# Delta rule: level products as pairs of 64x64 quarters of TensorE's array, on packed tiles

## The reference

```
m = where(strict, einsum('bhncd,bhnsd->bhncs', k_beta, k) * decay, 0.0)
t_inv = triangular_solve(eye + m, eye, lower=True, unit_diagonal=True)
u = t_inv @ v_beta
w = t_inv @ (k_beta * exp(g)[..., None])
```

## Time and profile before

| | |
|---|---|
| median of 3 runs | 1583.88 us (1583.28 to 1585.54) |
| profiled execution, own time | 1580.38 us |
| its span, first to last instruction | 1577.5 us |
| TensorE busy, share of the span | 97% |
| VectorE, ScalarE, GpSimd busy | 38%, 38%, 36% |
| granted TensorE clock, mean | 0.997 |

### The profile page before, as it was taken

The page is one execution under the profiler, slowest core; times in us unless marked ns, Lnnn a source line. Parts: engine busy times, 40 slices in busy tenths (PEclk is TensorE's granted clock), DMA queues, the critical chain, the costliest instruction groups (busy, mean ns, idle before and its releaser), DMA issues.

```text
span 1577.5 us, 21190 instructions
## 1 busy us (share of the span) xinstructions
PE 1534.2 (97%) x7900; PEld 1267.5 (80%) x7900; DVE 595.1 (38%) x996; ACT 603.7 (38%) x998; POOL 560.0 (36%) x270
## 2 busy tenths in 40 slices
PE   6889999999999999999999999999999999999998
PEld 6868888888887778888888887777688888888887
DVE  3355556565565422221022224566432222012210
ACT  5643444334442533322232234576433332223221
POOL 4522321323212244434533444221234444444442
PEclk9999999999999999999999999999999999999999
DMA  7411111111110133233323233111123332433322
GB/s 250 125 64 54 41 30 51 54 41 44 38 34 11 50 94 113 88 98 92 117 81 106 82 85 124 48 41 33 36 78 107 109 94 76 124 94 94 90 84 80
DMA packets 39218, 124.41 MB, mean 79 GB/s; under 512 B 4192, under 2 KB 5472, under 8 KB 39136
## 3 DMA queue, kind: packets, MB, share of 16 engines
q1 hardware_dynamic: 38976, 123.01, 25.5%
q10 hardware_dynamic: 160, 0.26, 0.1%
HBM read 120.89 MB, written 2.10 MB: 78 GB/s over the span
## 4 chain that ended last, share of the span: by engine, by line
PE 93%; DVE 3%; ACT 3%; issue 1%; DMA 0%; POOL 0%; SPq 0%; DVEq 0%; ACTq 0%
PE bank L564 72%; PE bank L730 3%; PE bank L717 3%; PE bank L728 2%; ACT ws L1091 2%; PE bank L1025 1%; DVE act_lo L1536 1%; PE bank L892 1%; PE bank L851 1%; DVE ws L1539 1%; PE bank L576 1%; PE bank L1049 1%; PE bank L738 1%; PE bank L881 1%; PE bank L764 1%
## 5 line engine op out<-in xcount | busy, mean ns | idle before, releaser
L511 POOL TENSOR_TENSOR w_lo<-w_raw,w_hi 128x1024 fp32r<-128x1024 f32 (+1 forms) x250 | 539.9, 2175 | 835.3 <-ACT w_hi L1091 835.1
L564 PE MATMUL bank<-act_hi,w_hi 128*128 128x512 f32 (+1 forms) x1776 | 708.3, 399 | 6.7 <-DVE act_lo L1536 2.7
L564 PE MATMUL bank<-act_hi,w_lo 128*128 128x512 f32 (+1 forms) x1776 | 680.1, 383 | 0.0
L564 PE MATMUL bank<-act_lo,w_hi 128*128 128x512 f32 (+1 forms) x1776 | 679.5, 383 | 0.0
L564 PEld LDWEIGHTS bank<-act_hi,w_hi 128*128 128x128 f32 x1776 | 335.4, 189 | 74.7 <-issue 13.5
L564 PEld LDWEIGHTS bank<-act_hi,w_lo 128*128 128x128 f32 x1776 | 334.7, 188 | 65.8
L564 PEld LDWEIGHTS bank<-act_lo,w_hi 128*128 128x128 f32 x1776 | 335.5, 189 | 62.2 <-issue 5.6
L1091 ACT ACTIVATE w_hi<-w_raw 128x1024 fp32r<-128x1024 f32 (+1 forms) x250 | 230.5, 953 | 88.8 <-PE bank L564 86.6
L1530 DVE TENSOR_TENSOR ws<-bank,ws 128x512 f32<-128x512 f32 x110 | 75.9, 690 | 336.2 <-PE bank L564 326.2
L1091 ACT ACTIVATE ws<-ws 128x512 f32<-128x512 f32 (+2 forms) x135 | 87.1, 647 | 154.6 <-DVE ws L1530 107.4
L1798 DVE TENSOR_TENSOR xT<-xT,bank 128x512 f32<-128x512 f32 (+1 forms) x48 | 33.0, 687 | 257.0 <-PE bank L564 257.0
(11 more groups left out here) (150 smaller groups left out, 1218.7 us busy)
## 6 DMA issues: line engine op xcount, KB each, us to landing
w_raw<-w_stream SPq DMA_DIRECT2D x154, 512.0 KB, 3.6
w_raw<-w_out SPq DMA_DIRECT2D x32, 384.0 KB, 3.1
w_raw<-w_down SPq DMA_DIRECT2D x32, 384.0 KB, 3.1
w_raw<-w_down SPq DMA_DIRECT2D x32, 320.0 KB, 3.2
ws<-x_in SPq DMA_DIRECT2D x1, 2048.0 KB, 8.8
ws<-mem_in SPq DMA_DIRECT2D x2, 512.0 KB, 4.7
out<-ws SPq DMA_DIRECT2D x1, 1024.0 KB, 4.2
sq_c<-squares_in SPq DMA_DIRECT2D x1, 768.0 KB, 7.1
```

The lines of the kernel that those rows point to most:

```text
L511: nc.gpsimd.tensor_tensor(w_lo[:, s, 0:width * P], w_raw[:, s, 0:width * P], w_hi[:, s, 0:width * P].bitcast(F32), ALU.subtract).then_inc( ...
L564: mm = nc.tensor.matmul(acc, wt[:, c % RING, wsl], at[:, act0(k0 + k), off:off + n], start=(start and k == 0 and m == 0), stop=(stop and k ...
```

## The change

The lower and upper 64 rows of a tile meet only in the last level. So in levels 1 to 5 M, T and Z of a tile consist of two diagonal blocks of 64x64, and the off-diagonal ones are zero. Now each block is a product of its own, on the quarter of the array that its rows and output rows give: 64 rows, 64 columns of weights and 64 streamed columns. The blocks are kept packed: the row `TT` holds in its first 256 columns the four turned copies, 64 columns each, with the upper block on partitions 0 to 63 and the lower one on 64 to 127, and in its second 256 columns Z in the same form. `PM` is packed likewise. The masks become 64 wide (`small`). The joined Z is written out into `ZZ` in level 5, by row halves. The last level computes only the off-diagonal block of Z, on the quarters off the diagonal (P: rows 0 to 63 to outputs 64 to 127; Z: rows 64 to 127 to outputs 0 to 63). The turned copy comes from products with the identity on quarters instead of transposes. ZZ is cleared once at the start, beside KBG.

In the diff "..." stands for lines that don't change.

```diff
@@ -86,8 +86,10 @@
-(IDENT, ONES, ONES64, TRIU, NEG_LOWER, LEVEL0) = range(6)
-N_SQ = 6 + LEVELS - 1
+HB = P // 2
+(IDENT, ONES, ONES64, TRIU, NEG_LOWER, SMALL) = range(6)
+SMALL_IDENT, SMALL_LEVEL0 = 0, 1
+N_SQ = SMALL + (1 + LEVELS) // 2
@@ -98,10 +100,10 @@
     out[:, NEG_LOWER] = np.where(r <= c, 0.0, -1e30)
-    out[:, LEVEL0] = (c == r + 1) & (r % 2 == 0)
-    for k in range(1, LEVELS):
-        b = 2 ** k
-        out[:, LEVEL0 + k] = (r // b % 2 == 1) & (c // b == r // b - 1)
+    r, c = r % HB, np.arange(HB)[None, :]
+    small = [r == c, (c == r + 1) & (r % 2 == 0)]
+    small += [(r // 2 ** k % 2 == 1) & (c // 2 ** k == r // 2 ** k - 1) for k in range(1, LEVELS - 1)]
+    out[:, SMALL:].reshape(P, -1)[:, 0:HB * len(small)] = np.concatenate(small, axis=1)
     return out
@@ -337,6 +339,24 @@
+        def small(i, tiles):
+            at = SMALL * P + HB * i
+            flat = sq_c[:].rearrange("p a c -> p (a c)")[:, at:at + HB]
+            return flat.unsqueeze(1).to_broadcast([P, tiles, HB])
+        def half_rows(q):
+            return slice(HB * q, HB * (q + 1))
+        def diag(i, t, r, c):
+            return ws[half_rows(r), i, P * t + HB * c:P * t + HB * (c + 1)]
+        def packed(i, t, r, second=0):
+            at = SEQ // 2 * second + HB * t
+            return ws[half_rows(r), i, at:at + HB]
         def over_tiles(i):
@@ -414,6 +434,16 @@
             return act_hi[P // 2 * half:P // 2 * (half + 1), 18, :]
+        PER_HEAD = 2 * (LEVELS - 3) + 3 * 2 + 2
+        def tz_count(k, g, first_only=False):
+            if k < LEVELS - 2:
+                return 2 * (k - 1) + g + 1
+            if k == LEVELS - 2:
+                return 2 * (LEVELS - 3) + 3 * g + (1 if first_only else 3)
+            return 2 * (LEVELS - 3) + 6 + g + 1
@@ -700,7 +730,11 @@
                 pe.wait_ge(S.dm_pre, h + 1)
-                transposes4(D[2], ZZ).then_inc(S.t_tr, 1)
+                for t in range(NT):
+                    for r in range(2):
+                        mm = nc.tensor.matmul(bank[half_rows(r), D[2], HB * t:HB * (t + 1)], packed(TT, t, r, 1),
+                                              sq_c[half_rows(r), IDENT, HB * r:HB * (r + 1)], start=True, stop=True)
+                mm.then_inc(S.t_tr, 1)
                 pe.wait_ge(S.qn_done, h + 1)
@@ -708,14 +742,20 @@
                     n = 12 * h + 2 * (k - 1)
+                    last = k == LEVELS - 1
                     for g in range(2):
...
                         else:
-                            pe.wait_ge(S.tz_done, n + g - 1)
+                            pe.wait_ge(S.tz_done, PER_HEAD * h + tz_count(k - 1, g, last))
                         for i, t in enumerate(half_tiles(g)):
-                            mm = nc.tensor.matmul(bank[:, D[3 - g], i * P:(i + 1) * P], tt(MM, t), tt(TT, t),
-                                                  start=True, stop=True)
+                            if last:
+                                mm = nc.tensor.matmul(bank[half_rows(1), D[3 - g], HB * i:HB * (i + 1)],
+                                                      diag(MM, t, 0, 1), packed(TT, t, 0), start=True, stop=True)
+                                continue
+                            for r in range(2):
+                                mm = nc.tensor.matmul(bank[half_rows(r), D[3 - g], HB * i:HB * (i + 1)],
+                                                      diag(MM, t, r, r), packed(TT, t, r), start=True, stop=True)
                         mm.then_inc(S.p_mm, 1)
@@ -723,16 +763,24 @@
                             pe.wait_ge(S.kdec_done, h + 1)
+                        if last:
+                            pe.wait_ge(S.tz_done, PER_HEAD * h + tz_count(k - 1, g))
                         for i, t in enumerate(half_tiles(g)):
-                            if k < LEVELS - 1:
-                                nc.tensor.matmul(bank[:, D[4 + g], i * P:(i + 1) * P], tt(ZZ, t), tt(PM, t),
-                                                 start=True, stop=True)
-                            mm = nc.tensor.matmul(bank[:, D[4 + g], (2 + i) * P:(3 + i) * P], tt(PM, t), tt(ZZ, t),
-                                                  start=True, stop=True)
+                            z_at = slice(P + HB * i, P + HB * (i + 1))
+                            if last:
+                                mm = nc.tensor.matmul(bank[half_rows(0), D[4 + g], z_at], packed(PM, t, 1),
+                                                      diag(ZZ, t, 1, 1), start=True, stop=True)
+                                continue
+                            for r in range(2):
+                                nc.tensor.matmul(bank[half_rows(r), D[4 + g], HB * i:HB * (i + 1)],
+                                                 packed(TT, t, r, 1), packed(PM, t, r), start=True, stop=True)
+                            for r in range(2):
+                                mm = nc.tensor.matmul(bank[half_rows(r), D[4 + g], z_at], packed(PM, t, r),
+                                                      packed(TT, t, r, 1), start=True, stop=True)
                         mm.then_inc(S.tz_mm, 1)
...
-                pe.wait_ge(S.tz_done, 12 * h + 12)
+                pe.wait_ge(S.tz_done, PER_HEAD * (h + 1))
                 pe.wait_ge(S.kbg_done, h + 1)
@@ -786,7 +834,7 @@
-            pe.wait_ge(S.rw_cols, 5)
+            pe.wait_ge(S.rw_cols, 6)
             pe.wait_ge(S.ba_copied, 1)
@@ -1254,11 +1302,11 @@
                 a(psum(D[0]), w(E0), ACT.Exp, scale=-0.5, bias=col("ln_q")).then_inc(S.rr_done, 1)
-                act.wait_ge(S.z_pre, h + 1)
+                act.wait_ge(S.z_pre, 2 * h + 2)
                 a(w(MM), psum(D[1]), ACT.Copy).then_inc(S.t_done, 1)
...
                 act.wait_ge(S.t_tr, h + 1)
-                a(w(TT), psum(D[2]), ACT.Copy).then_inc(S.t_done, 1)
+                a(w(TT)[:, 0:SEQ // 2], psum(D[2], SEQ // 2), ACT.Copy).then_inc(S.t_done, 1)
                 if due(h):
@@ -1627,7 +1675,8 @@
             V.memset(w(KBG), 0.0).then_inc(S.rw_cols, 1)
-            dve.wait_ge(S.rw_cols, 1)
+            V.memset(w(ZZ), 0.0).then_inc(S.rw_cols, 1)
+            dve.wait_ge(S.rw_cols, 2)
             dve.wait_ge(S.ba_g, 1)
@@ -1667,9 +1716,15 @@
                 dve.wait_ge(S.mt_done, h + 1)
-                mul(psum4(D[3]), psum4(D[1]), over_tiles(LEVEL0)).then_inc(S.z_pre, 1)
-                dve.wait_ge(S.z_pre, h + 1)
-                sub(w4(ZZ), over_tiles(IDENT), psum4(D[3])).then_inc(S.z_done, 1)
+                pair_c = "p (t c) -> p t c"
+                for r in range(2):
+                    own = half_rows(r)
+                    mul(bank[own, D[3], 0:SEQ // 2].rearrange(pair_c, t=NT),
+                        bank[own, D[1], :].rearrange(pair_c, t=NT)[:, :, HB * r:HB * (r + 1)],
+                        small(SMALL_LEVEL0, NT)[own]).then_inc(S.z_pre, 1)
+                dve.wait_ge(S.z_pre, 2 * h + 2)
+                sub(w(TT)[:, SEQ // 2:].rearrange(pair_c, t=NT), small(SMALL_IDENT, NT),
+                    psum(D[3], SEQ // 2).rearrange(pair_c, t=NT)).then_inc(S.z_done, 1)
                 dve.wait_ge(S.rr_done, 2 * h + 2)
@@ -1680,19 +1735,30 @@
                         dve.wait_ge(S.p_mm, n + g + 1)
-                        own = slice(SEQ // 2 * g, SEQ // 2 * (g + 1))
-                        mul(w(PM)[:, own].rearrange("p (t c) -> p t c", c=P),
-                            bank[:, D[3 - g], 0:SEQ // 2].rearrange("p (t c) -> p t c", c=P),
-                            sq_c[:, LEVEL0 + k:LEVEL0 + k + 1, :].to_broadcast([P, NT // 2, P])).then_inc(S.p_done, 1)
+                        own = slice(P * g, P * (g + 1))
+                        if k < LEVELS - 1:
+                            mul(w(PM)[:, own].rearrange(pair_c, c=HB), psum(D[3 - g], P).rearrange(pair_c, c=HB),
+                                small(SMALL_LEVEL0 + k, NT // 2)).then_inc(S.p_done, 1)
+                        else:
+                            cp(ws[HB:, PM, own], bank[HB:, D[3 - g], 0:P]).then_inc(S.p_done, 1)
                     for g in range(2):
                         dve.wait_ge(S.tz_mm, n + g + 1)
-                        own = slice(SEQ // 2 * g, SEQ // 2 * (g + 1))
-                        if k < LEVELS - 1:
-                            both = ws[:, TT:ZZ + 1, own]
-                            sub(both, both, bank[:, D[4 + g], :].rearrange("p (a c) -> p a c", a=2)
+                        own = slice(P * g, P * (g + 1))
+                        full = w4(ZZ)[:, NT // 2 * g:NT // 2 * (g + 1), :]
+                        if k < LEVELS - 2:
+                            both = w(TT).rearrange("p (f g c) -> p f g c", f=2, g=2)[:, :, g, :]
+                            sub(both, both, psum(D[4 + g], 2 * P).rearrange("p (f c) -> p f c", f=2)
                                 ).then_inc(S.tz_done, 1)
+                        elif k == LEVELS - 2:
+                            sub(w(TT)[:, own], w(TT)[:, own], psum(D[4 + g], P)).then_inc(S.tz_done, 1)
```

(8 more changed lines are left out.)

## The result

| | before | after |
|---|---|---|
| median of the runs, us | 1583.58 (1581.46 to 1585.54, 4 runs) | 1559.65 (1559.41 to 1560.31, 4 runs) |
| profiled execution, us | 1580.4 | 1560.3 |
| its span, us | 1577.5 | 1558.5 |
| its mean granted clock | 0.997 | 0.990 |

The ratio is 0.985, 95% interval 0.9833 to 0.9867: 23.9 us less. The forecast was 1557, with a range of 1540 to 1583.

What follows compares the result with a forecast made beforehand. TensorE, busy 97% of the span, was taken as the bound. Heads 0 to 6 give 20.3 us, head 7 6.5, the start costs 0.4: 26.4 off 1583.9 gives 1557.5, 1557; range 1540 to 1583.

Steps and rivals of the forecast that it cites:

- Slot: One quarter instruction, or two at once on the diagonal quarters: 0.057 us, 144 a head, 8.2 us.
- just fits: Full weight load fits beside a 128-column stream of 0.11 us, so half a load fits beside half a stream.
- rival 1: Quarters don't run side by side, or the engine can't be fed faster: slower, 1611 us; 18%.
- Excursion: Each stay in quarter shape between full-array instructions costs TensorE 0.34 us; 13 a head, 4.4 us.
- loads and drain: Division of the 0.34 us shape-change price: first loads of each shape 0.16, engine drain the rest.
- Head: Each of heads 0 to 6: 15.5 - 8.2 - 4.4 = 2.9 us less, seven heads 20.3.
- VectorE stays covered: In heads 0 to 6 VectorE's work, 2.2 us a level, stays hidden under TensorE's 3.4 us; no waits show.
- rival 3: VectorE's new pieces become the wait, TensorE stands 0.3 us a group; in half the groups 13 us, 1570; 9%.
- Head 7: Head without projection fills: levels 2.0 us for 3.3, six levels 12.5 instead of 19.4, 6.5 us less in all.
- Start: VectorE's one clearing of ZZ, next to that of KBG in the chain, adds 0.4 us.
- Rival 4: Clock falls to 1.2 GHz in the levels of head 7, slots double: 5 us more, 1562; 5%.
- the step to the median, +3.5 us: Whole kernel: the median of the runs lies 3.5 us above the profiled execution, 1583.9 against 1580.4.

Runs made afterwards that it cites:

- Experiment 1: Kernel after with the lower-quarter products of levels 1 to 5 left out: 1560.88 us.
- experiment 2: Kernel after with one projection instruction moved between the two halves of P, six more changes of shape and back a head: 1575.46 us.
- Experiment 3: Kernel after with both projection fills of a level joined behind TZ, so P and TZ stand next to each other: 1554.71 us.
- experiment 5: Kernel after with ZZ cleared by GpSimd instead of VectorE: 1560.45 us (1554.90 to 1561.29).
- experiment 6: Kernel before with only the last level changed to off-diagonal quarter products: 1584.04 us, ratio 0.9993.
- experiment 7: Kernel after repeated unchanged, first of two repeats: 1559.87 us.
- experiment 9: Kernel after with spare quarter products in head 7's waits, three pairs in each between P and TZ, one behind TZ: 1556.49 us.
- experiment 11: Kernel after with eight spare full-array products ahead of level 1 of head 7, its waits kept: 1560.09 us.
- experiment 4: Kernel after with each half group issuing all upper-quarter products first, then all lower ones, instead of in turn: 1571.37 us.

## Why the prediction was right

- **Slot.** 0.057 forecast, 0.058 measured. Experiment 1 shows that the pair overlaps in full. The reasoning from halves to quarters held. One reason for it was read wrongly: that a full load "just fits" beside a stream of 0.11 is not in the earlier trace rows, where a load shows 0.191 us. Loads overlap one another there, as those of 0.134 us do now at steps of 0.029. The rule of the Trainium skill, TensorEngine Tiling (Array Packing), Gotcha 1: PSUM Pressure, named beside rival 1, does not hold here: both quarters write one bank side by side, on different partitions, without loss. And the 62 ns a matmul that the Trainium skill, TensorE: Matmul & The Clock Gate, section "Wait — 56ns, not 53.3ns?", gives for hardware decoding off are no floor in this kernel: 0.12 us for four instructions are 0.029 each.
- **Excursion.** 0.34 forecast, 0.34 measured by adding six (experiment 2). How it divides into loads and drain (0.16 and 0.18 in the prediction) no run shows.
- **Head.** 2.9 us forecast, 2.96 measured, 20.7 for seven instead of 20.3.
- **VectorE stays covered.** Right; rival 3 did not occur. Experiment 3 shows how thin the case for the cover is: without it TZ waits as long as an excursion lasts.
- **Head 7.** Levels of 2.05 us for 2.0, all six 12.7 for 12.5. From the first use of Z in head 6 to that in head 7 it was 42.07 us and is 35.56, so the term of 6.5 us was right up to there.
- **Start.** 0.4 forecast, 0.05 measured. The step that failed is that clearing ZZ costs what clearing KBG shows in the chain: the copies that stand behind it end with GpSimd's operation, clearing or not (experiment 5).
- **Clock.** This is the step that was incomplete. By work alone the terms measured are 20.7 + 6.5 - 0.05 = 27.1 us, and the medians differ by 23.9. Rival 4 expected the fall in the levels of head 7, with 5% for it. It came behind them and cost 1.9 us. Others were not foreseen, in code that the change does not touch: at 60 to 66 us TensorE's starts lose 2.6 us against before, 0.4 near 20 us, and in the second layer 1.6 and 1.1. The largest of them, before and then after (columns as in the earlier trace rows):

```profile
56.00:68.00 12.00, 9.06 (x73) 8.60 (x72) 3.05 (x8) 6.57 (x11) 9.47 (x4) 1.00 0.40 130
```

```profile
56.00:68.00 12.00, 9.06 (x51) 8.54 (x50) 1.86 (x6) 5.38 (x10) 7.01 (x3) 0.72 0.38 132
```

  With the 1.9 behind head 7 they are 7.6 us in the profiled run, and 27.1 - 7.6 is the 19.5 by which its last matmul, counted from its first, comes earlier. The two profiled executions differ by 20.1 us; the medians differ by 23.9, since that of before lies 3.2 above its profiled execution and that of the kernel after 0.7 below. The profiled run of before was a lucky one (1580.4 with a mean clock of 0.997; the 17 runs taken beside experiments 5, 6, 7 and 9 had 0.994 to 0.997 and a median of 1584.2). So the sum was made against a run with few such stretches, and the step to the median, +3.5 us, was taken as if it applied to both kernels alike. The forecast of 1557 came out 2.7 us low for this reason, not by the terms of the work, whose sum came within 0.7 us. How near it came is partly luck, as no term stood for the clock outside head 7, and one program spreads over more than 5 us with it (experiments 5 and 6).

## What to carry to other kernels

Two diagonal quarters with 64 columns, issued in turn, cost as much as one: count pairs as slots, and set the sum against 0.34 us for each stay between full-array instructions. An estimate from these prices: a full product saves 0.10 us (0.22 less two slots), so a stay pays from four products on. P alone, with four, gains 0.1 us, TZ with eight 0.5. Before a wait is covered with work of another shape, compare the wait with the price of the change of shape: here they were equal. And when a change is worth 1%, read the granted clock of each execution beside its time, since a step of 5 us can be half-clock stretches in code that nobody touched.

## What was not expected of the hardware

- Quarters in one queue overtake each other, but not by eight instructions: blocks of four lost 0.05 us in a group, blocks of eight 0.19 in each half group.
- GpSimd's 2.4 us operation held a VectorE copy of 0.2 us until it ended, in the traces of three kernels, and did not hold a clearing, in one (experiment 5).
- The clock's falls to 1.2 GHz come mostly at the same places of a program from run to run, yet the one behind head 7 was absent in the profiles of three kernels with the same waits (experiments 3, 5 and 11) and there in those of two more (2 and 4). They cost the kernel after 0.4 to 2.6 us each against before, and one program spread from 1554.9 to 1561.3 us with them.
- With the lower quarters left out, the clock of the profiled run fell in head 7 itself, from 458 us for 20 us, earlier and three times longer than with all the work in place; slots there took 0.107 us.
